# Stick-breaking attention: the triangular sum of the softplus in two rounded passes, with the split made by GpSimd

## What is computed

```python
z = einsum('bthd,bshd->bhts', q, k) * d ** -0.5          # key s, query t
strict = s_idx < t_idx
log_beta = log_sigmoid(z)
log_one_minus = where(strict, log_sigmoid(-z), 0.0)
suffix = cumsum(log_one_minus, axis=3, reverse=True) - log_one_minus
w = where(strict, exp(log_beta + suffix), 0.0)
out = einsum('bhts,bshd->bthd', w, v)
```

## Time and profile before

| | |
|---|---|
| runs | 2786.65, 2792.48, 2793.74 us |
| span of the profiled execution | 2787.8 us |
| PE busy / DVE / ACT / POOL over the span | 93% / 52% / 44% / 8% |
| the stage of stick-breaking attention | from about 1948 to 2154 us of the span |
| in 1950 to 2155: PE / DVE / ACT / POOL busy | 184.7 / 145.2 / 140.7 / 1.6 us of 205 |

### The profile page before, as it was taken

The page is one execution under the profiler, slowest core; times in us unless marked ns, Lnnn a source line. Parts: engine busy times, 40 slices in busy tenths (PEclk is TensorE's granted clock), DMA queues, the critical chain, the costliest instruction groups (busy, mean ns, idle before and its releaser), DMA issues. The chain is left out here.

```text
span 2787.8 us, 42260 instructions
## 1 busy us (share of the span) xinstructions
PE 2585.8 (93%) x16411; PEld 2094.8 (75%) x16411; DVE 1441.4 (52%) x2384; ACT 1225.3 (44%) x2333; POOL 235.9 (8%) x300
## 2 busy tenths in 40 slices
PE   5999999999999999998889999899998999998787
PEld 3778987877778989877777888787333887797776
DVE  5213266666655513477775723420677546364762
ACT  6112344544444321166664532220666647333662
POOL 1000020010020000001100000000000010004720
PEclk8999999999999999999999999999999999998889
DMA  7430010000112011100002220011000221111012
GB/s 256 173 138 23 18 33 1 1 1 1 62 69 97 25 61 46 61 2 1 2 2 76 106 76 31 12 50 58 19 1 23 76 80 46 38 46 61 1 54 75
DMA packets 71124, 139.55 MB, mean 50 GB/s; under 512 B 2729, under 2 KB 37954, under 8 KB 70802
## 3 DMA queue, kind: packets, MB, share of 16 engines
q1 hardware_dynamic: 53856, 75.89, 8.0%
q0 software_dynamic: 16832, 60.90, 6.0%
q10 hardware_dynamic: 242, 0.07, 0.0%
HBM read 120.08 MB, written 16.78 MB: 49 GB/s over the span
## 5 line engine op out<-in xcount | busy, mean ns | idle before, releaser
L163 ACT ACTIVATE WORK<-PS 128x512 f32<-128x512 f32 (+5 forms) x315 | 156.4, 496 | 634.9 <-PE PS L795 390.4
L795 PE MATMUL PS<-HT_R,W_R 128*128 128x512 f32 (+1 forms) x896 | 332.4, 371 | 0.0
L794 PE MATMUL PS<-WORK_R,W_R 128*128 128x512 f32 (+1 forms) x736 | 270.3, 367 | 0.0
L793 PE MATMUL PS<-WORK_R,W_R 128*128 128x512 f32 (+1 forms) x672 | 248.7, 370 | 13.4 <-DVE W_R L163 7.2
L163 DVE TENSOR_REDUCE SM<-PS 128x1 f32<-128x1280 f32 (+3 forms) x180 | 199.1, 1106 | 93.9 <-PE PS L1107 48.2
L927 PE MATMUL PS<-WORK_R,HT_R 128*128 128x512 f32 x528 | 210.1, 398 | 8.6 <-DVE W_R L163 7.5
L795 PE MATMUL PS<-W_R,WORK_R 128*128 128x256 f32 (+3 forms) x704 | 214.6, 305 | 0.0
L928 PE MATMUL PS<-WORK_R,MIXT_R 128*128 128x512 f32 x544 | 214.0, 393 | 0.0
L858 PE MATMUL PS<-BASE,WORK 128*128 128x128 f32 (+1 forms) x1270 | 187.1, 283 | 26.8 <-DVE WORK L163 18.5
L929 PE MATMUL PS<-W_R,HT_R 128*128 128x512 f32 x528 | 207.4, 393 | 0.0
L794 PE MATMUL PS<-W_R,HT_R 128*128 128x256 f32 (+2 forms) x688 | 206.2, 300 | 0.0
(11 more groups left out here) (297 smaller groups left out, 5650.8 us busy)
## 6 DMA issues: line engine op xcount, KB each, us to landing
MIXT<-in_w_mod POOLq DMA_DIRECT2D x8, 2048.0 KB, 8.5
x_scratch<-WORK POOLq DMA_DIRECT2D x24, 512.0 KB, 2.9
WORK<-x_scratch POOLq DMA_DIRECT2D x24, 512.0 KB, 3.6
W<-in_odd_w_in SPq DMA_DIRECT2D x12, 1024.0 KB, 5.2
W<-in_o_w_in SPq DMA_DIRECT2D x10, 1024.0 KB, 5.3
W<-in_even_w_in SPq DMA_DIRECT2D x5, 2048.0 KB, 7.7
W<-in_w_mod SPq DMA_DIRECT2D x4, 2048.0 KB, 20.6
WORK<-in_x POOLq DMA_DIRECT2D x16, 512.0 KB, 7.9
```

The source lines that it names most:

```text
L163: self.last = Signalled(self, issue(*args, **kwargs))
L793: mm(out, a[0], b_[0], start=k == 0, stop=False)
L794: mm(out, a[1], b_[0], start=False, stop=False)
L795: return mm(out, a[0], b_[1], start=False, stop=k == KT - 1)
```

## The change

The sum against LOWER was one float32 product per head. Now POOL writes a rounded copy of SSP (SPH, "the cast") and the rest SSP minus SPH (SPL, "the subtraction"), both float32r, and PE makes two float32r products, one with each. The product of the high part stands ahead of the column totals, that of the low part behind them, and `logs_summed`, for which the weights wait, is signalled by the low one. The max that overwrites SSP waits for the subtraction of two blocks before, where it waited for the sums. The column totals still read SSP in float32. LOWER becomes float32r.

```diff
@@ places @@
-        LOWER = HT[:, 9216:9344]
+        LOWER = HT_R[:, 9216:9344]
+        SPH, SPL = [[WORK_R[:, o + 1024 * n:o + 1024 * n + 1024].rearrange("p (h c) -> p h c", h=2) for n in range(2)] for o in (14080, 16128)]
@@ stick_sums on PE @@
-                pe.wait_ge(sp_ready, n + 1)
+                pe.wait_ge(sp_high, n + 1)
                 for i in range(2):
-                    last = mm(z_at(n)[:, i, 0:w], LOWER, SSP[n % 2][:, i, 0:w], start=False, stop=True, skip_group_check=True)
-                last.then_inc(logs_summed, 1)
+                    mm(z_at(n)[:, i, 0:w], LOWER, SPH[n % 2][:, i, 0:w], start=False, stop=False, skip_group_check=True)
                 if n in decays:
...
                     last.then_inc(total_ready, 1)
+                pe.wait_ge(sp_low, n + 1)
+                for i in range(2):
+                    last = mm(z_at(n)[:, i, 0:w], LOWER, SPL[n % 2][:, i, 0:w], start=False, stop=True, skip_group_check=True)
+                last.then_inc(logs_summed, 1)
@@ stick_softplus on DVE @@
-                    dve.wait_ge(logs_summed, n - 1)
+                    dve.wait_ge(sp_low, n - 1)
@@ on POOL, ahead of the wait for the stage's end @@
+            def stick_split():
+                for n in range(len(blocks)):
+                    w = 512 - cols_of(n)
+                    sp, high, low = [a[n % 2][:, :, 0:w] for a in (SSP, SPH, SPL)]
+                    pool.wait_ge(sp_ready, n + 1)
+                    if n >= 2:
+                        pool.wait_ge(logs_summed, n - 1)
+                    nc.gpsimd.tensor_copy(high, sp).then_inc(sp_high, 1)
+                    pool.wait_ge(sp_high, n + 1)
+                    nc.gpsimd.tensor_tensor(low, sp, high, ALU.subtract).then_inc(sp_low, 1)
+
+                if b == 3:
+                    stick_split()
```

More of the change, by code:

```diff
@@ L276, in build @@
                                         "decay_out", "decayed_acc", "block_ready", "block_taken")]
-        lower_ready = sem("lower_ready")
+        lower_ready, sp_high, sp_low = [sem(f"stick_{n}") for n in ("lower_ready", "sp_high", "sp_low")]
         dve_to_pe = sem("dve_to_pe")
```

## The result

The changed kernel takes 2836.93 us (median of 4 runs, 2830.51 to 2838.07) against 2792.39 for the kernel before: ratio 1.016, interval 1.0146 to 1.0174, **44.5 us slower**. The direction and the waits of DVE behind POOL were forecast, the size was not: 2818.5 was given, with a range that ends at 2834.

A forecast was written before the change was run, and what follows sets the result against it. The prediction took a loop over PE's scores, DVE and ACT, not PE's own pace, as the bound. It summed 19.1 + 4 + 3 = 26 us onto the profiled 2787.8, giving 2814, or 2818.5 as median; range 2801 to 2834.

The forecast's parts named there:

- The bound: In the stage, a loop over scores, DVE's min and ACT's exp and weights sets the pace, 4.3 us a block.
- The cost on PE: Two float32r pairs hold PE for 1.26 us instead of 1.92 per 512-wide block; no gain in time was taken.
- The split: On POOL, per 1024 columns: cast 1.0 us, subtraction 2.37; low product ends 4.3 us after the max.
- DVE behind POOL: DVE's two-SBUF-operand decay and gate products wait for whole POOL instructions; delays at gate products sum to 19.1 us.
- both walked places: Two timeline places where a gate product waits for POOL's subtraction, making the next min 2.9 and 2.6 us late.
- the first kind: Place where the gate product meets the next block's subtraction: min 2.9 us late, counted three times, none at stage's end.
- All other blocks ... I take 1.0 a cycle, 4 in all: Blocks outside the walked places: decay products behind casts and late low products, 4 us, bounds 0 and 10.
- 3 for start and end: Split latency uncovered at the stage's start, 2.3 us, and some 0.8 us at its end.
- Rival 2: PE falls to half clock in the stage as well: 5 to 15 us more, 2823 to 2833 us; chance 0.15.
- Rivals 1, 3 and 4: 1: split only latency, 2801 us, chance 0.15; 3: PE bounds, 2776, 0.04; 4: idle covers all, 2785 to 2800, 0.06.

The follow-up runs named there:

- the kernel with the gate products replaced: The changed kernel with only the 8 gate products replaced by a sum over one SBUF operand of the same width; 2809.6 us, ratio 1.0067.
- Filler in those waits: The changed kernel plus two float32 zero-matrix products ahead of the low part in only the 7 iterations with a blocked gate product; 2830.92 us, ratio 1.0141.
- the single pair: The kernel before with its float32 sum replaced by one float32r pair on a constant tile, ahead of the totals (wrong data); 2795.17 us, ratio 1.0013.

## Why the forecast was wrong in size

*The bound.* Right. That PE's 90% is not the pace was read from its waits for ACT and the 0.3 us between sums and weights; one pair in place of the sums gained nothing.

*The cost on PE.* The pair was put at 0.63 us; the high pair at 2055.75 was followed by the totals at 2056.42, 0.67. That the part gains nothing alone was right, that it costs nothing was not: it costs 12 us, with the clock at 0.95. Of what the stage shows of it, 7.1 of 9.2 us, three blocks at half clock are the cause.

*The split.* Right: cast 1.04 us for 1.0, subtraction 2.366 for 2.37 where nothing holds it.

*DVE behind POOL.* Right in mechanism and at both walked places to 0.1 us (2.9 and 2.6). Over the stage the seven places add 3 x 2.9, 2.5, 2 x 2.6 and 2.2 us, 18.6 in all for 19.1. The count of kinds was a little off, since the first kind has a min behind it in the last pair too; it changes the sum by 0.3 us. Not foreseen was that the gate product's wait hangs on where it arrives: with the decay product gone from the wait it took 0.86 us on the mean, with the cast put behind the decay product still 1.71.

*"All other blocks ... I take 1.0 a cycle, 4 in all", and 3 for start and end.* Nearly right at full clock. In the kernel with the gate products replaced, the blocks outside the walked places add 9.9 us, of which 1.6 are half clock. That leaves 8.3: 2.5 at the start (2.3 forecast) and 5.8 in the rest (4 forecast). The end adds 1.0 (0.8 forecast). The 19 us by which that kernel is over before mustn't be set against these 7 us, since 7.0 of them lie in the walked places (the decay product's 0.8 and the like), where the walk had them already.

*The step that failed: the half clock had no term in the sum.* Rival 2 weighed it as another case with a chance of 0.15, when it follows from the forecast's own terms: stalls of 2.5 us a place are idle time of PE. With 18.6 for the places, 8.3 and 1.0 for the rest the stage would have grown by 27.9 us, for 26 forecast. It grew by 44.6, and the 17 us between are products at 1.2 GHz. Rival 2's own price was too low as well. It let a third of PE's longer work reach the end, "about a third, so 5 us"; measured are 15.2 of 19.2 us, about four fifths, since whole blocks at half clock lie on the loop. Its "5 to 15 us" put onto the sum would have given 2824 to 2834, so the range too was short at its upper end. The forecast did name the sign: it is wrong if the clock in the stage falls clearly below 0.99, and it fell to 0.87.

What isn't shown is why the clock falls at one place and not at another. The kernels without long waits at the gate products have 0.96 and 0.97. Filler in those waits took the changed kernel from 0.87 to 0.92, so these waits bring down part of it.

*Rivals 1, 3 and 4.* The latency alone is 12 us (9 forecast), seen when the two-operand products are gone; what little half clock that kernel has is in the 12. PE as the bound is excluded by the single pair, full cover by the time.

## What to carry to other kernels

Before work is moved to an idle GpSimd, list the DVE instructions with two operands in SBUF that run at the same time, and see what stands first in each queue when the release comes: an instruction queued directly behind the one that releases GpSimd loses as a rule (38 of the 40 decay products here took longer), and its delay can push the next one into a longer wait. A shorter matmul gains nothing where the waits of PE point to another engine, and may lose the full clock with the idle time that it makes. When a forecast contains new stalls of PE, the clock belongs into its sum and not among the rivals. And when effects are separated by leaving one out, compare block by block: a total for one effect can contain what the forecast has counted under another.

## What the runs showed of the hardware

- A POOL instruction can lose too: its subtraction took 2.80 us in place of 2.37 where the DVE product of 0.69 started 0.12 before it.
- A sum over one SBUF operand on DVE (686 ns for 512 columns) isn't stretched beside POOL; a product of two is (692 to 1435 ns).
- The granted clock alternated between its two levels in a stage in which PE was busy for 40 of 50 us and waited for ACT up to 3.5 us at a time. It stayed at 2.4 GHz in cycles in which PE was busy for 43.6 of 52 to 54 us and waited for 1.9 us at most. With 36.7 of 50 us in the kernel with one pair it was 0.97 in one cycle and 0.90 in the next, at the same order of work. What decides between the levels is not shown.
- At a granted clock of 0.53 on the mean the same 19 PE instructions were busy for 6.53 us in place of 3.80, and their block lasted 7.19 us in place of 4.46: the same 2.73 us more.
